# Two attention branches run as one pipeline of 32 heads, with the normalisation sums after the first up chunk

## The reference

```
q, k_slc, v_slc, k_win, v_win = heads of h @ w_in       # 16 query heads, 4 key/value heads, width 64
o_slc = softmax(mask(q k_slc^T / 8)) v_slc               # with 256 tokens every block is selected: causal attention
o_win = softmax(mask(q k_win^T / 8)) v_win               # window 512 > 256: causal attention
o     = g0 * o_cmp + g1 * o_slc + g2 * o_win             # g: sigmoid of 48 columns of h @ w_in
y_attn = o @ w_attn_out
x = x + (sigmoid(mg_rnn) * y_rnn + sigmoid(mg_attn) * y_attn) @ w_out
x = x + (gelu(conv(rms_norm(x) @ w_gate)) * ...(rms_norm(x) @ w_up)) @ w_down      # and two more such networks later
```

## Time and profile before

| | |
|---|---|
| median of 3 runs | 1275.49 us (1271.6 to 1280.0) |
| profiled execution, its own time | 1275.6 us |
| its span, first to last instruction | 1273.7 us |
| PE busy / DVE busy / ACT busy | 1198.8 / 932.4 / 679.9 us |
| mean granted TensorE clock | 0.976 |

### The profile page before, as it was taken

How to read it: one execution, slowest core, us unless ns; L and a number is a source line. 1 busy time by engine, 2 the same in 40 slices (tenths; PEclk the granted TensorE clock), 3 DMA queues, 4 the chain that set the end, 5 groups by cost and what they waited for, 6 DMA issues and landing times.

```text
span 1273.7 us, 25289 instructions
## 1 busy us (share of the span) xinstructions
PE 1198.8 (94%) x9597; PEld 1162.2 (91%) x9597; DVE 932.4 (73%) x1581; ACT 679.9 (53%) x1184; POOL 17.4 (1%) x14
## 2 busy tenths in 40 slices
PE   5997998998989999999999999999999799999996
PEld 5997998988979999999899899999998789999996
DVE  5777887466676898888868758777675886877665
ACT  5756764333354675555644456554564645655452
POOL 1000000000000100000000010000000100000000
PEclk9988998999999999999999999999998999999998
DMA  6564544322225476666464126666554313666560
GB/s 217 185 212 130 169 133 133 120 80 83 57 66 176 135 224 190 187 187 183 133 211 154 33 83 197 202 187 189 182 149 149 117 34 120 204 189 188 188 183 33
DMA packets 52780, 190.95 MB, mean 150 GB/s; under 512 B 5984, under 2 KB 5984, under 8 KB 52576
## 3 DMA queue, kind: packets, MB, share of 16 engines
q1 hardware_dynamic: 52416, 188.77, 47.6%
q10 hardware_dynamic: 288, 1.12, 0.2%
HBM read 188.82 MB, written 1.05 MB: 149 GB/s over the span
## 4 chain that ended last, share of the span: by engine, by line
PE 79%; DVE 11%; ACT 5%; issue 3%; DMA 2%; SPq 0%; DVEq 0%; ACTq 0%
PE bank L505 23%; PE bank L506 22%; PE bank L507 22%; DVE w_low L1385 3%; DMA w_raw<-weight_stream 2%; ACT w_high L1011 2%; PE bank L597 2%; PE bank L608 1%; PE bank L620 1%; PE bank L622 1%; PE bank L621 1%; PE bank L596 1%; PE bank L513 1%; PE bank L515 1%; PE bank L514 1%
## 5 line engine op out<-in xcount | busy, mean ns | idle before, releaser
L1385 DVE TENSOR_TENSOR w_low<-w_raw,w_high 128x1024 fp32r<-128x1024 f32 x356 | 434.6, 1225 | 180.6 <-ACT w_high L1011 177.0
L1011 ACT ACTIVATE w_high<-w_raw 128x1024 fp32r<-128x1024 f32 x356 | 375.1, 1058 | 338.2 <-PE bank L507 281.3
L505 PE MATMUL bank<-h_high,w_high 128*128 128x256 f32 x1824 | 523.3, 287 | 18.7 <-DVE h_low L1423 11.9
L506 PE MATMUL bank<-h_low,w_high 128*128 128x256 f32 x1824 | 514.5, 282 | 0.0
L507 PE MATMUL bank<-h_high,w_low 128*128 128x256 f32 x1824 | 513.5, 282 | 0.0
L505 PEld LDWEIGHTS bank<-h_high,w_high 128*128 128x128 f32 x1824 | 347.7, 191 | 22.4 <-issue 12.6
L506 PEld LDWEIGHTS bank<-h_low,w_high 128*128 128x128 f32 x1824 | 346.6, 190 | 0.6
L507 PEld LDWEIGHTS bank<-h_high,w_low 128*128 128x128 f32 x1824 | 346.5, 190 | 0.0
L505 PE MATMUL bank<-r_high,w_high 128*128 128x256 f32 x866 | 247.4, 286 | 16.1 <-ACT arena L1214 7.3
L506 PE MATMUL bank<-r_low,w_high 128*128 128x256 f32 x866 | 244.9, 283 | 0.0
L507 PE MATMUL bank<-r_high,w_low 128*128 128x256 f32 x866 | 244.4, 282 | 0.0
(11 more groups left out here) (206 smaller groups left out, 1180.2 us busy)
## 6 DMA issues: line engine op xcount, KB each, us to landing
w_raw<-weight_stream SPq DMA_DIRECT2D x356, 512.0 KB, 3.6
small<-small_in ACTq DMA_DIRECT2D x1, 1065.5 KB, 9.4
x<-x_in SPq DMA_DIRECT2D x4, 256.0 KB, 6.1
out<-arena SPq DMA_DIRECT2D x4, 256.0 KB, 2.5
small<-small_in ACTq DMA_DIRECT2D x1, 30.0 KB, 4.1
```

The lines of the kernel that those rows point to most:

```text
L505: mm(out_ap, wh, high, start=start, stop=False, skip_group_check=True)
L506: mm(out_ap, wh, low, start=False, stop=False, skip_group_check=True)
L1011: fn(w_high[:, c % RING, :], w_raw[:, c % RAW, :], ACT.Copy).then_inc(high_ready, 1)
L1385: v.tensor_tensor(w_low[:, c % RING, :], w_raw[:, c % RAW, :], f(w_high[:, c % RING, :]), ALU.subtract).then_inc(low_ready, 1)
```

## The change

The two runs of the first block's attention become one call over 32 heads (`count`), i = 0 to 31: head i uses query head i % 16 and branch i // 16. The waits between the runs go away; what is left between head 15 and head 16 is what stands between any two heads. DVE's `output` gets a wait for its own output of four groups earlier.

The ten merge-gate tiles move: their 20 halves stand behind the steps in `MG_AT`, that is 0, 1, then 4 to 19, then 32 and 34. `MG_LATE` names for each finished tile the step in which DVE scales it and ACT splits the ring's next chunk: 2, 6, 8, 10, 12, 14, 16, 18, 20, and 35, behind the last step. DVE makes the low part one step later than ACT the high part, and `after` stands behind `output` where it stood ahead of it.

At the end, PE no longer waits for all four low parts of the turned output before "ao" but for each as it comes to it, and its wait for the scaled gates stands behind "ao". The last tile's split (ACT behind `output_high`, DVE behind `output_low`) stands between the outputs and the sigmoids.

In all three feed-forward networks `norm_sums` stands behind the first up chunk. The two later attentions keep their order, with the new signature.

```
-        MG_PER_BRANCH = (SIZE["mg"] - MG_EARLY) // 2
-        MG_START = (8, 2)
-        def mg_late(h, n):
-            ...
+        MG_AT = (0, 1, *range(4, 20), 32, 34)
+        MG_LATE = {MG_AT[2 * j + 1] + 1: MG_EARLY + j for j in range(SIZE["mg"] - MG_EARLY)}
...
                         last.then_inc(chunk_used, 1)
-                        if j == 0 and which == 0:
+                        if j == 0 and which == 1:
                             norm_sums(2 * n + 1)
...
-            def banks_free_0():
-                if n == 0:
-                    pe.wait_ge(cmp_done, 4)
-                else:
-                    pe.wait_ge(probs_copied, NH)
-                    pe.wait_ge(o_read, 4)
-
-            for n in range(2):
-                attention(n, lambda h, t: q0[:, h // 2, t * P:(t + 1) * P],
-                ...
-            pe.wait_ge(mg_scaled, 16)
-            turn_output(0, o0)
-            for k in range(0, DT, 2):
-                turned(0)(k)
-            column_tiles("ao", r_high, r_low)
-
-            pe.wait_ge(acc_read, 4 * ACC_YR + 4)
+            def merge_between(i):
+                if i in MG_AT:
+                    at = MG_AT.index(i)
+                    merge_gates(MG_EARLY + at // 2, (at % 2,))
+
+            attention(0, 2 * NH, lambda i, t: q0[:, i % NH // 2, t * P:(t + 1) * P],
+                      ...
+                      lambda: pe.wait_ge(cmp_done, 4), between=merge_between)
+            turn_output(0, o0)
+            column_tiles("ao", r_high, r_low, turned(0))
+            pe.wait_ge(mg_scaled, 16)
...
+            attention(0, 2 * NH, probs0, merge_gate)
             output_high(0)
+            merge_gate(2 * NH + 3)
             act.wait_ge(mg_scaled, 16)
...
+                    if gated:
+                        if 4 * g >= NH:
+                            dve.wait_ge(o_read, g - 3)
...
+                for i in range(count + 3):
                     if before:
-                        before(h)
+                        before(i)
+                    if i < count:
+                        row_max(i)
+                    if 2 <= i < count + 2:
+                        copy_turned(i - 2)
+                    if i >= 3 and i % 4 == 2:
+                        output((i - 3) // 4)
                     if after:
-                        after(h)
-                    if h >= 3 and h % 4 == 2:
-                        output((h - 3) // 4)
+                        after(i)
...
+            def merge_split(i):
+                if i - 1 in MG_LATE:
+                    split_low(BASE["mg"] + MG_LATE[i - 1] + RING)
+
+            attention(0, 2 * NH, o0, probs_t0, gated=True, before=merge_gate, after=merge_split)
+            merge_gate(2 * NH + 3)
             output_low(0)
+            merge_split(2 * NH + 4)
```

More of the change, by code:

```diff
@@ L586, in norm_sums, with attention, scores @@
                 ins.then_inc(sumsq_ready, 1)
-            def attention(n, q, kpad, v, probs, probs_t, banks_free, before=None, between=None):
-                def scores(h):
+            def attention(n, count, q, kpad, v, probs, probs_t, banks_free, before=None, between=None):
+                done = NH * n
+                def scores(i):
                     if before:
-                        before(h)
-                    if h >= 3 or n == 1:
-                        pe.wait_ge(probs_ready, NH * n + max(h - 2, 0))
-                    b = bank[h % 3]
-                    mm(b[:, 0:P], q(h, 0), kpad(h)[:, 0:P], start=True, stop=False, skip_group_check=True)
-                    mm(b[:, P:3 * P], q(h, 1), kpad(h), start=False, stop=False, skip_group_check=True)
+                        before(i)
+                    if i >= 3:
+                        pe.wait_ge(probs_ready, done + i - 2)
+                    b = bank[i % 3]
+                    mm(b[:, 0:P], q(i, 0), kpad(i)[:, 0:P], start=True, stop=False, skip_group_check=True)
+                    mm(b[:, P:3 * P], q(i, 1), kpad(i), start=False, stop=False, skip_group_check=True)
                     mm(b[:, :].rearrange("p (a c) -> p a c", c=2 * P)[:, :, 0:P], ident_b[:, :],
@@ L1445, in scaled, with attention, row_max @@
                 v.tensor_tensor(dst, tile(name, i), rstd[:, :], ALU.mult).then_inc(tile_free["dve"], 1)
-            def attention(n, o, probs_t, branch=None, before=None, after=None):
-                def row_max(h):
-                    dve.wait_ge(scores_ready, NH * n + h + 1)
-                    b = bank[h % 3]
+            def attention(n, count, o, probs_t, gated=False, before=None, after=None):
+                done = NH * n
+                def row_max(i):
+                    dve.wait_ge(scores_ready, done + i + 1)
+                    b, h = bank[i % 3], i % NH
@@ L1468, in output @@
+                def output(g):
+                    dve.wait_ge(pv_done, done + 4 * g + 4)
+                    heads = slice(4 * g % NH, 4 * g % NH + 4)
+                    w = weights_o[:, :, heads]
+                    link(v.reciprocal(w, sums[:, :, heads]))
+                    if gated:
+                        link(v.tensor_tensor(w, w, nsa_gate[:, :, heads, 1 + 4 * g // NH], ALU.mult))
+                    dst = o[:, :, heads, :]
                     src = bank[5 + g % 2][:, :].rearrange("p (t h d) -> p t h d", t=TT, h=4)
@@ L1477, in attention @@
+                for i in range(count + 3):
                     if before:
-                        before(h)
-                    if h < NH:
-                        row_max(h)
-                    if 2 <= h < NH + 2:
-                        copy_turned(h - 2)
+                        before(i)
+                    if i < count:
+                        row_max(i)
+                    if 2 <= i < count + 2:
+                        copy_turned(i - 2)
+                    if i >= 3 and i % 4 == 2:
+                        output((i - 3) // 4)
```

141 lines of the change are left out of this document (56 added, 85 removed).

## The result

The changed kernel takes 1247.1 us (median of 6 runs, 1237.7 to 1251.6) against 1273.2 us of the kernel before on the same chip: a ratio of 0.977 with a 95% interval of 0.9747 to 0.9796. Forecast were 1258.7 us and a range from 1254 to 1268, so the change gained 26 us where 16.9 were forecast. The profiled execution after took 1250.9 us, 24.7 us less than the one before.

The account below looks back on a forecast made before the run. PE, busy for 94% of the span, was taken to bound the kernel; 11.6 us (attention stage), 1.7 (clock behind it) and 3.6 (networks' heads) make 16.9, so 1275.6 becomes 1258.7 us, range 1254 to 1268.

Parts of the forecast that it names:

- Part 8: Networks' heads: the up chunk fills three waits of 1.3 us ahead of the sums, 0.3 comes back; gain 3.6 us.
- Parts 1 to 3 and 5: Attention stage, first scores to first "ao" matmul: 89.35 us against 100.97, a gain of 11.6 us.
- Part 5: Stage's end: turned output taken piece by piece, "ao" starts 3.75 us after the last head's product, with no further wait.
- Parts 2 and 3: Halves at steps 0, 1 remove the 2.02 us starting wait; those at 32, 34 fill gaps; plain heads wait 2.3 us.
- Part 4: DVE's split one head later: DVE's waits for ACT's high part, 8.0 us in all, go, but PE never felt those between gated heads.
- Part 6: "ao" behind the attention stage: the low clock after idle time goes, gain 1.7 us, bounds 0 and 1.7.
- Part 7: Behind the stage: late sigmoids make DVE's `merged` start 2.8 us late, hidden from PE by chunks split ahead.
- E: Plain heads: the 2.3 us of waits don't come and a dip elsewhere goes too, 1254 us or less; chance 0.07.
- A: Networks' heads: late splits make PE wait again, gain given back, 1262.3 or 1266.8 us; chance 0.16.
- B: Steps 24 to 32: each of three waits brings a 1.6 us clock dip, up to 4.8, 1263.5 us; chance 0.06.
- C: "ao" and "wo" run at DVE's merging and splitting pace, only the networks' gain stays, 1272.0 us; chance 0.06.
- D: Twelve plain heads run at low clock, 1279.8 us, or 1330.7 with the gated heads too; chance 0.05.

Follow-up runs that it names:

- e13: Kernel before, the three networks' sums of squares taken over a constant in their old place, so PE need not wait for DVE's norm; 1258.5 us, ratio 0.986.
- e14: Changed kernel with five useless DVE additions ahead of the norm's last one in the three networks, so PE waits at the sums again; 1263.1 us, ratio 0.9909.
- e1: Kernel before with only the three networks' sums of squares moved behind the first up chunk; 1270.0 us, ratio 0.9947.
- e2: Changed kernel with the sums of squares put back behind the first gate chunk, leaving only the attention's part; 1262.6 us, ratio 0.990.
- e4: Changed kernel with PE again waiting for all four low parts of the turned output before "ao"; median 1251.6 us, ratio 0.982.
- e8: Changed kernel with the 20 gate halves in one row behind steps 4 to 23, none at 0, 1, 32 and 34; median 1255.2 us, ratio 0.983.
- e3: Changed kernel with DVE's split in the same step as ACT's, the last one ahead of `output_low`; median 1262.5 us, ratio 0.988.
- e9: Kernel before with two useless float32 matmuls behind the first up chunk of each network; 1275.4 us, ratio 1.0003.
- e15: Kernel before with two useless float32 matmuls behind each network's first up chunk and two already fulfilled waits ahead of them; 1275.5 us, ratio 0.9989.
- e11: Changed kernel with the sums of squares in the middle of the first up chunk, the second run of that version; 1244.3 us, ratio 0.974.

## Why the prediction was wrong

The step that failed is Part 8, and with it the sum, in what they left out: PE's matmul time behind the sums of squares was taken as unchanged, a term put at nothing without a reason. Part 8 took the three waits at the sums for worth their length (3 x 1.3, with bounds of 3.9 and a loss of 0.6). Behind sums for which PE stood, all three networks ran at the slow pace, 4% more per matmul than at the fast one. Taking away those 1.2 us opened the way for another 6.7 to 7.4 us in each network behind, which came in some executions and not in others; e13 and e14 show this for the wait alone, at both places. The sum also took the parts as independent. Each half alone came near its forecast, e1 3.7 us (3.6) and e2 11.1 by the medians (13.3), so the waits themselves were sized right; the 10 us of pace came on top, and not in e1. That the wait keeps the networks slow is shown; why its removal alone, in e1, gives the fast pace so seldom stays open. The forecast's 1258.7 is about what the change gives without a fast stretch: the profiled 1250.9 and its 10.7 us of pace make 1261.6. The timeline rounds both paces' durations to 0.28 us, as in the earlier trace rows, and only 124 matmuls of that trace had the fast one.

- *Parts 1 to 3 and 5:* 89.34 us against 89.35. The heads took 85.74 (forecast 85.6) with 1.3 us of waits for copies, not 2.3; other small gaps made up for it, so the agreement to 0.01 is luck in part. "ao" began 3.60 us after the last product (3.75). Inside, e4 gives Part 5 its 1.9 us. By e8, Parts 2 and 3 are worth 2.4, nearly all of it the 2.0 at the start; the halves at 32 and 34 bring little.
- *Part 4* was put at nothing and is worth 2.8 us, by e3: PE does feel the split at the first gated heads and at the last. That it was hidden in between is right.
- *Part 6:* 1.7 us came, and went back with e4's longer idle time.
- *Part 7:* DVE waited 3.1 us for the sigmoids (forecast 2.8) and PE felt nothing.
- *Part 8:* the waits alone gave 1.41 us at each head, less 0.3 behind the first one: 1.1 + 1.4 + 1.4 = 3.9 against 3.6. The 0.3 at the first down chunk was 0.2 us after a slow beginning and 0.5 after a fast one; what it does to the pace was not seen. In the whole change the term is worth 3.9 plus 0 to 14 us of pace.
- *Rivals:* E had the right side and the wrong reason. A, B, C and D did not occur. The rule of the Trainium skill behind D (TensorE: Matmul & The Clock Gate, "A second HAM failure mode: psum-queue depth-cycling") would have slowed the plain heads; no profile here shows it, the clock stayed at 1.00 over all 32 heads.

What stays open: why a float32 pass after standing still leaves the slow pace, why one wait at a down chunk ended the fast pace seven times of seven and a longer one ahead of a gate chunk did not, why the networks of e1 got it so seldom and those of the changed kernel and of e13 so often, and why "ao" and "wo" differ between executions. The traces show one difference ahead of the sums, of 3 ns. PE came to 30 of the 33 at the slow pace; where the first sum's matmul then started 118 or 119 ns after the last product's, 20 of 23 networks began fast, and where it started 115 ns after it, none of 7. It can't be the whole cause, since the useless matmuls of e9 and e15 started 118 or 119 ns after theirs in five of six cases, and the pace behind them stayed slow. No run here sets this step on its own.

## What to carry to other kernels

Compare the count of matmuls in equal full windows, and not only waits: the same code at the same granted clock can run at two paces, and an edit in one place can change which one a stretch elsewhere gets. When a kernel's times spread by more than its clock explains, count these stretches before believing a ratio, and read a part's worth from its own stage. Small waits of PE at the head of a long loop deserve more care than their length says; sums taken half a chunk later than before, so that nothing is waited for on either side, gave the fastest version here (e11).

## What the runs showed of the hardware

128x256 matmuls with a weight load each started 117.8 or 113.3 ns apart at a granted clock of 1.00, duration 279 to 281 or 276 ns in the records, with a pace held for up to some 1650 matmuls. The networks' 4700 or so matmuls have 21 us between all slow and all fast (4700 x 4.47 ns). Of the low clock: PE's longest idle time around the attention stage was 0.9 us after the change, and the clock stayed at 1.00. With 2.21 in e4, behind a stage that had been full, the next 5.1 us had a mean clock of 0.67; the 2.02 us of e8, at the start of the heads, were followed by no fall.
